# Turned outputs and half of the turned keys: VectorE with 32x32 blocks and transfers through scratch memory in place of TensorE

## The reference, cut to what matters

```python
def step(S, inp):                      # one chunk; heads of width 128
    ...
    o_intra = jnp.einsum('bhij,bjhv->bihv', A, vc)
    S_new = jnp.exp(Lc)[..., None] * S + jnp.einsum(
        'bjhk,bjhv->bhkv', kc * jnp.exp(Lc[:, None] - L), vc)
    return S_new, o_inter + o_intra
...
yb = rms_norm(o, o_norm_g).astype(x.dtype).reshape(B, T, WIDTH_B) * jax.nn.silu(zb)
g_a, g_b = jnp.split(jax.nn.sigmoid(h @ w_merge + b_merge), 2, axis=-1)
y = g_a * (ya @ w_proj_a) + g_b * (yb @ w_proj_b)
out = x + gate * (y @ w_out)
```

## Time and profile before

| | before |
|---|---|
| three executions | 1557.94, 1558.01, 1558.31 us |
| span of the profiled execution | 1555.9 us |
| time of the profiled execution around its span | not listed by itself; the median is 2.1 us above the span |
| TensorE busy | 98% of the span |
| chain of waits, share of TensorE | 95% |
| DMA, share of 16 engines | 33.4% on SyncE's queue |
| mean granted TensorE clock | 0.996 of full |

### The profile page before, as it was taken

One profiled execution on the slowest core, in us unless ns is written; L12 is line 12 of the kernel. 1 busy time (PEld: TensorE's weight loads), 2 busy tenths in 40 slices (PEclk: granted clock), 3 DMA queues, 4 the chain that ended last, 5 costly groups with the idle time before them and its releaser, 6 DMA issues.

```text
span 1555.9 us, 31655 instructions
## 1 busy us (share of the span) xinstructions
PE 1527.1 (98%) x13048; PEld 1243.0 (80%) x13048; DVE 787.0 (51%) x1900; ACT 540.7 (35%) x1119; POOL 826.0 (53%) x1074
## 2 busy tenths in 40 slices
PE   5999999999999999999999999999999999999998
PEld 2777788877888788888779878888888978888886
DVE  4767464234558866232544774622453775623132
ACT  4334324334322532434331452243432353143330
POOL 0525434557863643365773472437786363437671
PEclk9999999999999999999999999999999999999999
DMA  9612211334453321233343231223544231222351
GB/s 339 243 55 83 83 57 55 111 133 158 168 197 108 110 70 57 82 109 108 137 164 135 92 120 43 83 66 114 208 154 149 75 110 56 78 72 91 102 167 60
DMA packets 62790, 178.94 MB, mean 115 GB/s; under 512 B 7086, under 2 KB 18695, under 8 KB 61864
## 3 DMA queue, kind: packets, MB, share of 16 engines
q1 hardware_dynamic: 62648, 176.93, 33.4%
HBM read 162.84 MB, written 11.96 MB: 112 GB/s over the span
## 4 chain that ended last, share of the span: by engine, by line
PE 95%; DVE 3%; DMA 1%; SPq 1%; issue 1%; ACT 0%; DVEq 0%
PE ps_D L758 56%; PE ps_D L755 25%; PE ps_XCD L820 2%; PE ps_XB L896 1%; PE ps_XB L949 1%; PE ps_XA L954 1%; PE ps_XA L921 1%; PE ps_XA L932 1%; PE ps_XB L948 1%; PE ps_XA L896 1%; DMA th_t<-in_w_ada 1%; SPq L507 1%; PE ps_XB L932 0%; PE ps_XCD L831 0%; PE ps_XCD L939 0%
## 5 line engine op out<-in xcount | busy, mean ns | idle before, releaser
L1702 POOL TENSOR_TENSOR w_lo_t<-w_raw,w_hi_t 128x256 fp32r<-128x256 f32 x920 | 681.0, 775 | 599.7 <-ACT w_hi_t L980 599.4
L758 PE MATMUL ps_D<-h_hi_t,w_hi_t 128*128 128x512 f32 x1024 | 411.2, 402 | 0.0
L758 PE MATMUL ps_D<-h_hi_t,w_lo_t 128*128 128x512 f32 x1024 | 399.6, 390 | 0.0
L758 PE MATMUL ps_D<-h_lo_t,w_hi_t 128*128 128x512 f32 x1024 | 399.5, 390 | 0.0
L980 ACT ACTIVATE w_hi_t<-w_raw 128x1024 fp32r<-128x1024 f32 x232 | 240.0, 1051 | 124.6 <-PE ps_D L755 61.6
L758 PEld LDWEIGHTS ps_D<-h_hi_t,w_hi_t 128*128 128x128 f32 x1024 | 192.3, 188 | 46.3 <-issue 8.9
L758 PEld LDWEIGHTS ps_D<-h_hi_t,w_lo_t 128*128 128x128 f32 x1024 | 192.2, 188 | 41.8
L758 PEld LDWEIGHTS ps_D<-h_lo_t,w_hi_t 128*128 128x128 f32 x1024 | 192.6, 188 | 36.5
L755 PE MATMUL ps_D<-w_hi_t,h_hi_t 128*128 128x384 f32 (+1 forms) x384 | 141.6, 369 | 1.0 <-DVE yf_t L1342 1.0
L755 PE MATMUL ps_D<-w_lo_t,h_hi_t 128*128 128x384 f32 (+1 forms) x384 | 136.6, 356 | 0.0
L755 PE MATMUL ps_D<-w_hi_t,h_lo_t 128*128 128x384 f32 (+1 forms) x384 | 136.3, 355 | 0.0
(11 more groups left out here) (386 smaller groups left out, 2332.9 us busy)
## 6 DMA issues: line engine op xcount, KB each, us to landing
w_raw<-in_w_blocks SPq DMA_DIRECT2D x232, 512.0 KB, 3.4
xr<-in_x_prompt SPq DMA_DIRECT2D x16, 512.0 KB, 5.0
x_or_AT<-in_x_prompt SPq DMA_DIRECT2D x14, 512.0 KB, 4.8
out_dram<-xr SPq DMA_DIRECT2D x12, 512.0 KB, 2.8
x_or_AT<-in_x_turned SPq DMA_DIRECT2D x3, 1024.0 KB, 5.6
p_or_hf<-in_x_turned SPq DMA_DIRECT2D x3, 1024.0 KB, 6.2
out_dram<-xr SPq DMA_DIRECT2D x8, 256.0 KB, 2.0
ibtok<-vtok SPq DMA_DIRECT2D x8, 192.0 KB, 3.5
```

The lines of the kernel that those rows point to most:

```text
L758: ins = mm(bank[:, :], w[:, s0, k0 + k, :], a[:, k, :], start=go, stop=end)
L1702: ins = g_.tensor_tensor(w_lo[:, c, k:k + 2], w_raw[:, n % NRAW, k:k + 2], f32(w_hi[:, c, k:k + 2]), ALU.subtract)
```

## The change: what it does

The four `yT` tasks of TensorE and VectorE and the `KT` tasks of tiles 2 and 3 go. In their place a half of `kk` (two tiles, 128 partitions x 1024 numbers) is turned in 32x32 blocks in place by one VectorE instruction, written to a scratch array in memory (`zk`, `zo`) by one transfer, and read back by four transfers, one for each group of 32 partitions, that put the blocks in their places. The pieces of the read-back are runs of 32 numbers, 128 bytes. Keys of tiles 2 and 3 come back to `k_turned`, outputs of tiles 0, 1 and of tiles 2, 3 to the two `o_turned`, which lie over `acc`/`kst` and over `qq`. `onorm` is cut in two (halves 60 and 64). A VectorE task `yD` (halves 65, 66, 69, 70) does the gate multiplication from SBUF; ScalarE's and GpSimd's part of `yT` stands at halves 66, 67, 70, 71. The squares' unused output goes to a slot of `yf` in place of `acc`.

```diff
+KEYS_TURNED = (1,)
+O_AT, ON_AT, YD_AT, YT_AT = (57, 59, 61, 63), (60, 64), (65, 66, 69, 70), (66, 67, 70, 71)
+KS_AT, KL_AT, OS_AT, OL_AT = (28, 28), (29, 29), (31, 33), (32, 34)
...
-        put(it, 28 + _t, 0, "KT", _t, "XC")
-        put(it, 28 + _t, 1, "o", _t, "XB")
-        put(it, 28 + _t, 1, "st", _t, "XA")
-    put(it, 32, 0, "onorm", 0)
+        if _t // 2 not in KEYS_TURNED:
+            put(it, 28 + _t, 0, "KT", _t, "XC")
+        at_half(it, O_AT[_t], "o", _t, "XB")
+        at_half(it, O_AT[_t], "st", _t, "XA")
+    for _r in KEYS_TURNED:
+        at_half(it, 56, "kD", _r)
+    for _r in range(2):
+        at_half(it, ON_AT[_r], "onorm", _r)
     for _t in range(NT):
-        at_half(it, 67 + _t, "yT", _t, "XB" if _t % 2 else "XA")
+        at_half(it, YD_AT[_t], "yD", _t)
+        at_half(it, YT_AT[_t], "yT", _t)
...
-        acc = sb("acc_t", [P, TB])
-        kst = sb("kst_t", [P, HB, P])
+        acc_kst = sb("acc_or_kst", [P, 2 * TB])
+        acc, kst = acc_kst[:, 0:TB], acc_kst[:, TB:].rearrange("p (h n) -> p h n", h=HB)
...
+        k_turned = first.enter_context(nc.sbuf_tensor("k_turned", [P, 2, HB, 2, P], F32))
...
+        o_turned = [t.rearrange("p (h t n) -> p h t n", h=HB, t=2)
+                    for t in (acc_kst[:, :], qq.rearrange("p h n -> p (h n)")[:, 0:1024])]
+        zk, zo = (nc.dram_tensor(f"z_{n}", [2, 4, 32, 2 * HB, 4, 32], F32).ap() for n in "ko")
...
+                for r in range(2):
+                    if r in KEYS_TURNED:
+                        later.setdefault(b0 + KS_AT[r], []).append(("ks", it, r))
+                        later.setdefault(b0 + KL_AT[r], []).append(("kl", it, r))
+                    later.setdefault(b0 + OS_AT[r], []).append(("os", it, r))
+                    later.setdefault(b0 + OL_AT[r], []).append(("ol", it, r))
...
+                half = slice(256 * a, 256 * a + 256)
+                if what == "ks":
+                    s.wait_ge("kD", len(KEYS_TURNED) * it + KEYS_TURNED.index(a) + 1)
+                    s.wait_ge(f"kt_in{a}", 64 * it)
+                    load(zk[a].rearrange("i q (h t) j p -> (i q) h (t j p)", t=2), kk[:, :, half], f"kz{a}")
+                elif what == "kl":
+                    s.wait_ge(f"kz{a}", 16 * (it + 1))
+                    for j in range(4):
+                        load(k_turned[32 * j:32 * j + 32, a].rearrange("p h t (i c) -> p (h t) i c", c=32),
+                             zk[a, :, :, :, j].rearrange("i q n p -> q n i p"), f"kt_in{a}")
+                elif what == "os":
+                    s.wait_ge("oD", 2 * it + a + 1)
+                    s.wait_ge(f"ot_in{a}", 64 * it)
+                    load(zo[a].rearrange("i q (h t) j p -> (i q) h (t j p)", t=2), kk[:, :, half], f"oz{a}")
+                elif what == "ol":
+                    s.wait_ge(f"oz{a}", 16 * (it + 1))
+                    s.full(it, "o" if a else "st", 3 if a else 1)
+                    for j in range(4):
+                        load(o_turned[a][32 * j:32 * j + 32].rearrange("p h t (i c) -> p (h t) i c", c=32),
+                             zo[a, :, :, :, j].rearrange("i q n p -> q n i p"), f"ot_in{a}")
...
-                    s.freed(it, "KT", a)
+                    if a < 2:
+                        s.freed(it, "KT", a)
+                    else:
+                        s.wait_ge("kt_in1", 64 * (it + 1))
                     for h in range(HB):
-                        ins = mm(bank[:, P * h:P * h + P], kst[:, h, :], ibtok[:, a, P * h:P * h + P],
+                        left = kst[:, h, :] if a < 2 else k_turned[:, 1, h, a % 2, :]
+                        ins = mm(bank[:, P * h:P * h + P], left, ibtok[:, a, P * h:P * h + P],
                                  start=True, stop=True)
-                elif task == "yT":
-                    s.wait_ge("on", 4 * it + a + 1)
-                    for h in range(HB):
-                        ins = tr(bank[:, P * h:P * h + P], kk[:, h, P * a:P * a + P], ident[:, :])
...
+                    if a // 2 in KEYS_TURNED:
+                        s.wait_ge(f"kz{a // 2}", 16 * (it + 1))
+                    s.wait_ge("yl", 16 * it + 4)
                     fn(kk[:, :, P * a:P * a + P], bank[:, 0:512].rearrange("p (h n) -> p h n", h=HB), ACT.Copy)
                     for h in range(HB):
-                        ins = fn(acc[:, P * h:P * h + P], bank[:, P * h:P * h + P], ACT.Square,
+                        ins = fn(yf[:, 1, P * h:P * h + P], bank[:, P * h:P * h + P], ACT.Square,
...
-                                s.freed(it, "yT", a)
+                                s.full(it, "st", 3)
+                                s.wait_ge("yt", 4 * it + a + 1)
...
+                elif task == "kD":
+                    half = kk[:, :, 256 * a:256 * a + 256]
+                    do(v.transpose(half, half), "kD")
                 elif task == "onorm":
-                    s.freed(it, "o", 3)
-                    do(ts(oss, oss, 1.0 / P, EPS, ALU.mult, ALU.add))
-                    rsqrt(orst, oss, ow1, ow2)
-                    for t in range(NT):
+                    s.freed(it, "o", 2 * a + 1)
+                    c, half = slice(8 * a, 8 * a + 8), kk[:, :, 256 * a:256 * a + 256]
+                    do(ts(oss[:, c], oss[:, c], 1.0 / P, EPS, ALU.mult, ALU.add))
+                    rsqrt(orst[:, c], oss[:, c], ow1[:, c], ow2[:, c])
+                    for t in (2 * a, 2 * a + 1):
                         o = kk[:, :, P * t:P * t + P]
-                        s.done(tt(o, o, orst[:, HB * t:HB * t + HB].unsqueeze(2).broadcast_to([P, HB, P]), ALU.mult), "on")
-                elif task == "yT":
-                    s.full(*key)
-                    free(stt(yf_slot(16 * it + 4 + a), bank[:, 0:512].rearrange("p (h n) -> p h n", h=HB), og_half[:, 0:1],
-                             szb[:, :, P * a:P * a + P], ALU.mult, ALU.mult), *key)
+                        s.done(tt(o, o, orst[:, HB * t:HB * t + HB].unsqueeze(2).broadcast_to([P, HB, P]), ALU.mult))
+                    s.settle()
+                    do(v.transpose(half, half), "oD")
+                elif task == "yD":
+                    s.wait_ge(f"ot_in{a // 2}", 64 * (it + 1))
+                    do(stt(yf_slot(16 * it + 4 + a), o_turned[a // 2][:, :, a % 2], og_half[:, 0:1],
+                           szb[:, :, P * a:P * a + P], ALU.mult, ALU.mult), "yt")
```

More of the change, by code:

```diff
@@ L258 @@
         + [f"w_in{n}" for n in range(NRAW)] + ["w_hi", "w_lo", "burst", "th_full", "kk", "sq", "ssq", "qa", "k_sc",
-           "lvl", "dgp", "at0", "smax", "p_exp", "p_norm", "kst", "on", "yf", "yh", "yl", "y7f", "y7h", "y7l", "x_in0", "x_in1", "xst", "rstd",
+           "lvl", "dgp", "at0", "smax", "p_exp", "p_norm", "kst", "kD", "kz0", "kz1", "kt_in0", "kt_in1", "oD", "oz0", "oz1", "ot_in0", "ot_in1", "yt", "yf", "yh", "yl", "y7f", "y7h", "y7l", "x_in0", "x_in1", "xst", "rstd",
            "xn", "xm", "xh0", "xh1", "h_hi", "h_lo", "grow", "s_rows", "s_th", "s_sq8", "s_sc", "s_exp", "s_p", "ckv", "s_oT",
@@ L392, in build @@
         ps_s = kst[0:8]
-        AT32 = kst[:, :, :].rearrange("p h (t i) -> p (h t) i", t=NT)
+        AT32 = kst.rearrange("p h (t i) -> p (h t) i", t=NT)
         sq_in = ibS[:, 0:256]
@@ L406, in build @@
         first.close()
+        k_turned = first.enter_context(nc.sbuf_tensor("k_turned", [P, 2, HB, 2, P], F32))
+        first.close()
+        first = ExitStack()
         yb_hi, yb_lo = sb("yb_hi_t", [P, 4, TB], F32R), sb("yb_lo_t", [P, 4, TB], F32R)
@@ L563, in event @@
             def event(what, it, a):
-                if what == "xst":
+                half = slice(256 * a, 256 * a + 256)
[18 more added lines that the diff above has]
+                             zo[a, :, :, :, j].rearrange("i q n p -> q n i p"), f"ot_in{a}")
+                elif what == "xst":
                     s.full(it, "o", 3)
@@ L1126, in side @@
                     s.full(*key)
-                    if it or a:
-                        s.full(*((it, "st", a - 1) if a else (it - 1, "st", 3)))
-                    s.free(fn(kst[:, :, :], bank[:, :].rearrange("p (h n) -> p h n", h=HB), ACT.Copy), *key)
+                    if a:
+                        s.full(it, "st", a - 1)
+                    s.free(fn(kst, bank[:, :].rearrange("p (h n) -> p h n", h=HB), ACT.Copy), *key)
                 elif task == "o":
```

## The result

The changed kernel takes 1580.9 us (median, 1580.1 to 1581.2), the kernel before beside it 1558.2 us: ratio 1.0145, interval [1.0131, 1.0159]. It is slower by 1.45%, with 1578.0 predicted. The profiled execution took 1580.85 us with a span of 1578.7 us, 22.8 more than the 1555.9 before.

The account below looks back on a forecast made before the run. TensorE, busy 98%, was taken as the bound: 1555.9 span + 2.1 around it - 11.7 transposes + 26.0 waits + 5 clock + 0.7 iteration 0 = 1578.0 us. Likeliest case 1567 to 1594; wider range 1556 to 1603.

Parts of the forecast that it names:

- TensorE is the bound, so removed transposes are gained in full: TensorE: two KT tasks at 0.46 us and four yT at 0.50 go per iteration, 11.7 us in all.
- VectorE's block transposes are hidden: VectorE: three transposes per iteration, about 1.35 us each, fit in idle time; only iteration 0 is allowed 0.7 us.
- Keys hidden: Keys of tiles 2 and 3, before st 2: write, weight load and read-back have about 20 us, so no wait.
- Order alone, 3.1 us an iteration: At pb0: the last yb_lo behind GpSimd's weight split makes TensorE wait 3.1 us even if transfers cost nothing.
- The read-back's landing: Outputs' second half: load lands 3.4 us after issue, read-back runs 4.6 behind it; pb0 then waits 6.1 us.
- The write is hidden: SyncE's queue: read-back waits behind ga4's weight load anyway; x tiles add some 0.3 us (iteration 2), about 1.3 (iteration 1).
- From landing to pb0, 7.2 us: After the read-back lands: gate multiplication, yb_hi, evacuation, both splits and last yb_lo in a row, 7.2 us.
- The clock, 5 us: TensorE's clock falls behind pb0's waits: 2 us a fall, 6 chances in 10 for each of four; bounds 0 and 11.
- rivals, 3 and 4: Slow 128-byte read-back packets: about 40 ns each, 1603 us, chance 0.12; or 95 ns, 1710 us, chance 0.03.
- Rival 2: At pb0: read-back lands by 1415.4, so only the order's 3.1 us wait remains; 1558.7 us, chance 0.10.
- Rival 1: At pb0: transfers and GpSimd's last piece are in time, only the removal counts; 1546.3 us, chance 0.13.
- rival 4: Strided read-back many times slower: 95 ns a packet, 24 us a half, keys late too; 1710 us, chance 0.03.

Follow-up runs that it names:

- e3_both: Changed kernel with the last yb_hi/yb_lo piece ahead of pa2's weight split, and write and read-back of the outputs' second half one unit earlier: 1549.0 us, ratio 0.9945.
- e7_keys: e3_both with the keys of tiles 2 and 3 turned on TensorE again, without their block transpose, write or read-back: 1552.5 us, ratio 0.9965.
- e2_early: Changed kernel with only write and read-back of the outputs' second half one unit earlier in SyncE's queue: 1564.8 us, ratio 1.0050.
- e9_xbehind: Changed kernel with the two x tiles' loads behind the read-back of the outputs' second half in SyncE's queue: 1570.2 us, ratio 1.0089.
- e5_big_order: e1_order with the outputs' read-back in runs of 4 KB in place of 128 bytes, blocks not put into place: 1558.1 us, ratio 0.9998.
- e8_xonly: Changed kernel with the two x tiles' loads between write and read-back of the outputs' second half (a misplaced edit): 1583.1 us, ratio 1.0159.
- e1_order: Changed kernel with only the last yb_hi/yb_lo piece back ahead of pa2's weight split on ScalarE and GpSimd: 1563.6 us, ratio 1.0040.

## Why the prediction was right, point by point

- *TensorE is the bound, so removed transposes are gained in full.* Right: laid side by side, the products of e3_both and of the kernel before give 0.48 to 0.50 us a task, 11.9 in all for 11.7; e7_keys gives the keys' part as 3.6 for 3.7.
- *VectorE's block transposes are hidden.* Right; 1.35 us was expected for one, and 1.25 measured (below). In iteration 0, 1.3 us at an output product (L989) in place of the 0.7 allowed, and at the place that the prediction named. Its chain in the kernel after: TensorE waits for ScalarE's squares, and ScalarE had idled 11.9 us for VectorE's reduction for the sample rows, which now stands behind the first half's scales and block transpose and starts at 271.22, where it started at 266.44:

```profile
271.54 0.87 ACT L1140 ACTIVATE smS<-smS,bm_half 128x8 f32<-128x8 f32 x4 [11.90 <-DVE smS L1453]
```

- *Keys hidden.* Right: TensorE's waits show none for `k_turned`.
- *Order alone, 3.1 us an iteration.* Right: 3.19 in three iterations, 2.01 in iteration 1 (e2_early), 11.6 in all for 12.4.
- *The read-back's landing.* The mechanism was right, its size too large: from ga4's weight load to landing 3.4 + 4.6 = 8.0 us predicted, 6.6 measured (1428.94 to 1435.51). The two terms were added as if the read-back's packets began when the load had landed; they overlap. That alone takes iteration 3 from 6.1 to 4.7.
- *The write is hidden.* Right in iteration 0 and, but for 0.2 us, in 3; wrong in 1 and 2: the prediction priced the x tiles at 1.3 and 0.3 us there without a working, e9_xbehind shows 3.4 and 2.9. What it left out is when the write behind them lands, which is what releases the read-back (in iteration 2 it goes out 7.4 us after the write, where 4.4 are needed in iteration 3). All waits together: 21.9 for 26.0.
- *From landing to pb0, 7.2 us.* 7.15.
- *The clock, 5 us.* The term that was mis-sized: 11.2 measured, past the upper bound of 11. It had 2 us a fall and 6 chances in 10; the clock fell all four times, and one fall cost 2.6, 3.0, 3.1 and 2.5 us. The prediction's own working from the earlier trace rows gives 2.7 us of lost work, close to these; it then took 2 without a reason. Four times 2.7 is 10.8.

So the mechanism was right, but that 1578.0 came within 3 us of 1580.9 is partly luck, because two errors cancel: 4.1 us too much of waits, 6.2 too little of clock; the 0.6 of iteration 0 is most of the rest. Of the rivals, 3 and 4 (slow small packets; no row gave their 40 and 95 ns) are excluded by e5_big_order and by the read-back itself, 6.0 us from first issue to landing in iteration 3 of the kernel after. Rival 2 (order alone) is e2_early's kernel: it was put at 1558.7 and takes 1564.8, since it too left out the clock. Rival 1 (only the removal counts) was 1546.3, and e3_both reaches 1549.0 once both places of the order are mended.

The Trainium skill (VectorE: DVE Perf Modes, The three transpose paths), of which rival 4 was the case, calls a plain strided copy 19 times slower than the crossbar's for a large innermost stride of the destination; with the innermost 32 numbers together on both sides, no such factor is seen here: 0.45 us in 5.7 is what the small runs cost.

## What to carry to other kernels

Work that leaves a saturated engine is gained only if the detour's whole chain still ends in time: ask of each transfer what releases its issue, what lands ahead of it, and what a later consumer's engine does between landing and use. Here three entries of the order tables, one step each (the last piece on ScalarE and GpSimd, the write and its read-back on SyncE), turn +1.45% into -0.6% with the same instructions. And where TensorE is the bound, price a wait of several microseconds not at its length but at its length plus what the clock takes behind it: here half as much again in the changed kernel, and from 0.28 (e8_xonly) to 0.57 (e1_order) of the waits in the others where it fell.

## What the runs showed of the hardware that was not expected

- The clock: of the waits up to 2.0 us at pb0 none was followed by a slower clock (0.4, 0.7, 0.8, 0.9, 0.9, 1.3, 1.4, 2.0, 2.0); one of 2.2 was, one of 3.0 was, of three of 3.19 two were, and every one of 4.1 or more. The stretch at 0.50 was 6.8 us long at three waits of the changed kernel and 10.2 at the longest; in e8_xonly and e9_xbehind it was only 3.4 at waits of 4.2, 4.6, 4.8 and 4.5. What one fall took from the work behind the wait lay between 1.6 and 3.1 us and didn't grow with the wait (1.6 behind 9.3 us, 2.6 behind 4.1). On what it depends no run shows.
- GpSimd and VectorE slow each other when they run side by side on SBUF. In iteration 3 of the changed kernel:

```profile
1420.65 3.72 POOL L1753 TENSOR_TENSOR w_lo_t<-w_raw,w_hi_t 128x256 fp32r<-128x256 f32 x4 [5.32 <-ACT w_hi_t L1021]
...
1431.53 2.82 POOL L1753 TENSOR_TENSOR w_lo_t<-w_raw,w_hi_t 128x256 fp32r<-128x256 f32 x4 [1.38 <-ACT w_hi_t L1021]
```

  The first split has VectorE's gate multiplications beside it, the second has not: 0.9 us more. The same multiplication shows the other side, and beside it stands the block transpose (lines by form, after):

```profile
L1608 DVE SCALAR_TENSOR_TENSOR yf_t<-acc_or_kst,og_half,qT_or_szb 128x512 f32<-128x512 f32 x8 | 8.2, 1030 | 3.3 <-DMA acc_or_kst<-z_o 3.1
...
L1608 DVE SCALAR_TENSOR_TENSOR yf_t<-qq,og_half,qT_or_szb 128x512 f32<-128x512 f32 x8 | 6.0, 752 | 48.2 <-DMA qq<-z_o 48.1
...
L1605 DVE STREAM_TRANSPOSE kk<-kk 128x1024 f32<-128x1024 f32 x8 | 10.0, 1245 | 0.3
```

  1030 ns where a split runs beside it, 752 where GpSimd is idle. It is not the tile: in e2_early the two multiplications from `qq` in iteration 3 have a split beside them and take 1.90 us, that split 3.73, where they take 1.54 in the kernel after. The change made this pairing, since the multiplication now reads SBUF twice and no longer PSUM. The Trainium skill (GPSIMD Engine Reference, Specifications) names it, contention of GpSimd with VectorE's instructions that have two SBUF inputs. The trace agrees. GpSimd's splits over the whole kernel stay at 681 us, so it is local.
- A transfer of 1024 runs of 128 bytes holds SyncE's queue for about 0.9 us, one of 32 runs of 4 KB for 0.4, but the landing is nearly the same.
